# Attention weights turned in four quarters of 32 rows, both pairs at the beginning of each round, with a third place for turned weights

## The reference, cut to what matters

```
s = einsum('bnqkgd,bnskd->bnkgqs', q, kb) * (HEAD_DIM_2 ** -0.5)
s = where(mask, s + bias, NEG_INF_2)
m = maximum(max(s, axis=-1), sink)
p = exp(s - m)
p = p / (sum(p, axis=-1) + exp(sink - m))
o = einsum('bnkgqs,bnskd->bnqkgd', p, vb)
return o * silu(gate)
```

## Time and profile before

| | us |
|---|---|
| median of three runs | 1177.78 |
| lowest and highest | 1177.29, 1177.83 |
| the profiled execution | 1178.13 |
| its span, from the first to the last instruction | 1176.3 |
| TensorE busy | 1164.8 |
| VectorE busy | 676.3 |
| GpSimd busy | 456.2 |
| ScalarE busy | 358.3 |

### The profile page before, as it was taken

How to read it: one execution, slowest core, us unless ns; L and a number is a source line. 1 busy time by engine, 2 the same in 40 slices (tenths; PEclk the granted TensorE clock), 3 DMA queues, 4 the chain that set the end, 5 groups by cost and what they waited for, 6 DMA issues and landing times.

```text
span 1176.3 us, 16568 instructions
## 1 busy us (share of the span) xinstructions
PE 1164.8 (99%) x6255; PEld 950.7 (81%) x6255; DVE 676.3 (57%) x1249; ACT 358.3 (30%) x720; POOL 456.2 (39%) x437
## 2 busy tenths in 40 slices
PE   9999999999999999999999999999999999999997
PEld 6888888888888878887878788888988887777786
DVE  5645557333277403067777874894698335555568
ACT  7312122100011212545674631241111134443322
POOL 3424222233342224354666765304224224454534
PEclk9999999999999999999999999999999999999999
DMA  8321121443212122301114241232111220142113
GB/s 240 116 73 45 36 81 36 129 151 120 95 36 72 64 72 81 100 25 27 46 42 133 64 172 62 84 131 66 50 62 39 65 67 1 37 161 83 37 37 143
DMA packets 75072, 93.53 MB, mean 80 GB/s; under 512 B 13937, under 2 KB 54089, under 8 KB 74482
## 3 DMA queue, kind: packets, MB, share of 16 engines
q1 hardware_dynamic: 67270, 88.73, 22.7%
q10 hardware_dynamic: 7724, 3.74, 1.2%
HBM read 75.11 MB, written 18.92 MB: 80 GB/s over the span
## 4 chain that ended last, share of the span: by engine, by line
PE 96%; DVE 1%; POOL 1%; issue 1%; ACT 0%; DVEq 0%; POOLq 0%; ACTq 0%
PE bank L890 24%; PE bank L892 23%; PE bank L891 23%; PE bank L1183 4%; PE bank L1162 3%; PE wide L1176 2%; PE wide L1352 2%; PE bank L1130 1%; PE bank L1119 1%; PE bank L1326 1%; PE wide L892 1%; PE wide L891 1%; PE wide L890 1%; PE wide L1339 1%; PE bank L1107 1%; PE wide L1326 1%
## 5 line engine op out<-in xcount | busy, mean ns | idle before, releaser
L661 POOL CAST whi<-wraw 128x2048 fp32r<-128x2048 f32 x31 | 58.7, 1894 | 453.5 <-PE bank L892 403.7
L890 PE MATMUL bank<-u_hi,wlo 128*128 128x512 f32 x488 | 190.4, 390 | 0.0
L892 PE MATMUL bank<-u_hi,whi 128*128 128x512 f32 x488 | 189.9, 389 | 0.0
L891 PE MATMUL bank<-u_lo,whi 128*128 128x512 f32 x488 | 189.9, 389 | 0.0
L663 POOL TENSOR_TENSOR wlo<-wraw,whi 128x2048 fp32r<-128x2048 f32 x32 | 153.1, 4785 | 3.0 <-ACT whi L2429 0.5
L890 PE MATMUL bank<-x_hi,wlo 128*128 128x512 f32 x312 | 123.4, 395 | 0.0
L892 PE MATMUL bank<-x_hi,whi 128*128 128x512 f32 x312 | 121.6, 390 | 0.0
L891 PE MATMUL bank<-x_lo,whi 128*128 128x512 f32 x312 | 121.5, 389 | 0.0
L890 PEld LDWEIGHTS bank<-u_hi,wlo 128*128 128x128 f32 x488 | 91.6, 188 | 19.8 <-POOL wlo L663 0.8
L892 PEld LDWEIGHTS bank<-u_hi,whi 128*128 128x128 f32 x488 | 91.6, 188 | 19.1
L891 PEld LDWEIGHTS bank<-u_lo,whi 128*128 128x128 f32 x488 | 91.6, 188 | 18.9
(11 more groups left out here) (375 smaller groups left out, 2450.8 us busy)
## 6 DMA issues: line engine op xcount, KB each, us to landing
wraw<-in_w_in SPq DMA_DIRECT2D x26, 1024.0 KB, 5.4
wraw<-in_w_out SPq DMA_DIRECT2D x12, 1024.0 KB, 5.1
xr<-in_x SPq DMA_DIRECT2D x8, 512.0 KB, 7.2
hst<-in_x SPq DMA_DIRECT2D x4, 1024.0 KB, 5.0
hpool<-hst SPq DMA_DIRECT2D x4, 1024.0 KB, 4.2
smz<-mzs SPq DMA_DIRECT2D x16, 256.0 KB, 2.0
h<-hpool SPq DMA_DIRECT2D x4, 1024.0 KB, 7.6
resid<-h SPq DMA_DIRECT2D x8, 512.0 KB, 2.6
```

The lines of the kernel that those rows point to most:

```text
L661: g_.tensor_copy(whi[w % 2][:, :, :], wraw[:, :, :]).then_inc(s["w_hi"], 1)
L890: pe.matmul(ps, al, bh, start=(k == 0), stop=False)
L891: pe.matmul(ps, ah, bl, start=False, stop=False)
L892: return pe.matmul(ps, ah, bh, start=False, stop=(k == nk - 1))
```

## The change

Four things are edited, all in the attention.

- **Quarters.** `turn_p` makes of each 128 x 128 square four transposes of 32 rows, in four row groups, to the banks 0, 1, 6 and 7. Each of these banks holds both pairs of a round (columns 0 to 255 the even pair, from 256 the odd one). Banks 0 and 1 are now one tensor `both`; ScalarE's copy reads `both`, VectorE's reads `wide1` (banks 6 and 7). A copy still moves 384 (or 256) columns. `weigh` reads the turned weights in four runs of 32 columns (`pT_of`).
- **Both pairs at the beginning of each round**, in all rounds, on TensorE, VectorE and ScalarE. Both copies wait until both pairs are turned (`t_pt`), and the scores of the next even and odd pair wait until ScalarE and VectorE have copied both pairs.
- **A third place** for turned weights: places go by x % 3 (`turned_place`), so a copy waits for the weighing of the pair three before. The new places are `pTd` and `pTe`.
- **Order within a round.** VectorE does both `row_scale` right behind the scores, ahead of `side_out` and `low_y2`. ScalarE does both `weights` ahead of `side_out` and `high_y2`. GpSimd scales both pairs and splits weights behind them.

```diff
-        yp_lo, cc, ym_lo, x2_lo, y2c, _c, pTc = region(
+        yp_lo, cc, ym_lo, x2_lo, y2c, pTe, pTc = region(
...
-        bank = [ctx.enter_context(nc.psum_tensor(f"bank{i}", [P, 512], F32)) for i in range(4)]
+        both = ctx.enter_context(nc.psum_tensor("both", [P, S], F32))
+        bank = [both[:, 0:512], both[:, 512:S]]
+        bank += [ctx.enter_context(nc.psum_tensor(f"bank{i}", [P, 512], F32)) for i in range(2, 4)]
...
+        def turned_place(x):
+
+            if x % 3 == 0:
+                return pT
+            return ((pTb, pTd) if x < 16 else (pTc, pTe))[x % 3 - 1][:, :, HALF:HALF + BAND]
 
         def turned_half(x, half):
 
-            nb = pair(x)[4]
-            both = pT if x % 2 == 0 else (pTb if x < 16 else pTc)[:, :, HALF:HALF + BAND]
-            return both[:, :, 0:nb * P].rearrange("p i (b h c) -> p h i b c", h=2, c=64)[:, half]
-
-        def turned_bank(x, ps):
-
-            nb = pair(x)[4]
-            return ps[:, 0:2 * nb * 64].rearrange("p (i b c) -> p i b c", i=2, c=64)
+            n = 64 * pair(x)[4]
+            return turned_place(x)[:, half, 0:2 * n].rearrange("p (q m) -> p q m", q=2)
+
+        def turned_banks(x, half):
+
+            n = 64 * pair(x)[4]
+            pairs = (both, wide[1])[half][:, :].rearrange("p (q m) -> p q m", q=2)
+            return pairs[:, :, 256 * (x % 2):256 * (x % 2) + n]
+
+        def pT_of(x, i, b):
+
+            n = pair(x)[4]
+            rows = turned_place(x)[:, :, 0:128 * n].rearrange("p h (q m c) -> p h q m c", q=2, c=32)
+            return rows[:, :, :, i * n + b, :]
...
-            for x in range(32):
-                scale_p(x)
-                if x + 2 < 32:
-                    sinks(x + 2)
-                if x < 4:
-                    split_part(W_Q1, x)
-                elif 8 <= x < 16 and x % 2:
-                    split_part(W_O2, (x - 8) // 2)
-                elif x >= 16 and x % 2:
-                    split_part(W_O2 + 1 + (x - 16) // 8, x % 8 // 2)
+            for x0 in range(0, 32, 2):
+                for x in (x0, x0 + 1):
+                    scale_p(x)
+                    if x + 2 < 32:
+                        sinks(x + 2)
+                if x0 < 4:
+                    split_part(W_Q1, x0)
+                    split_part(W_Q1, x0 + 1)
+                elif 8 <= x0 < 16:
+                    split_part(W_O2, (x0 - 8) // 2)
+                elif x0 >= 16:
+                    split_part(W_O2 + 1 + (x0 - 16) // 8, x0 % 8 // 2)
...
-                base = (6, 4)[x % 2] if x < 16 else (0, 6)[x % 2]
-                halves = [take(base + half, ("a_pT", "v_pT")[half], x + 1) for half in range(2)]
+                if x % 2 == 0:
+                    for half in range(2):
+                        for q in range(2):
+                            take(6 * half + q, ("a_pT", "v_pT")[half], x + 2)
                 for i in range(2):
                     pe.wait_ge(s["g_nm"], 2 * x + i + 1)
                     for b in range(nb):
-                        for half in range(2):
-                            rows, c = slice(64 * half, 64 * half + 64), (i * nb + b) * 64
-                            mm = pe.transpose(halves[half][:, c:c + 64],
+                        c = 256 * (x % 2) + 32 * (i * nb + b)
+                        for q in range(4):
+                            rows = slice(32 * q, 32 * q + 32)
+                            mm = pe.transpose(bank[(0, 1, 6, 7)[q]][:, c:c + 32],
                                               sp[rows, x % 2, i, BAND - (nb - b) * P:BAND - (nb - b - 1) * P],
-                                              cst[rows, C_ID + 64 * half:C_ID + 64 * half + 64])
+                                              cst[rows, C_ID + 32 * q:C_ID + 32 * q + 32])
...
                 turn_p(x0)
-                if x0 >= 16:
-                    turn_p(x0 + 1)
+                turn_p(x0 + 1)
                 if x0:
                     weigh(x0 - 2)
                     weigh(x0 - 1)
                 if x0 + 2 < 32:
                     pair_scores(x0 + 2)
                     pair_scores(x0 + 3)
-                if x0 < 16:
-                    turn_p(x0 + 1)
                 if x0 == 16:
                     pe.wait_ge(s["v_y2lo"], 8)
                 for x in (x0, x0 + 1):
...
-                        ve.wait_ge(s["t_pt"], 2 * x - 2)
+                        ve.wait_ge(s["t_pt"], 4 * x - 4)
...
-                ps = filled(ve, "t_pt", 2 * x + 2, "v_pT", x + 1)
-                if x >= 2:
-                    ve.wait_ge(s["t_pv"], x - 1)
-                ve.tensor_copy(turned_half(x, 1), turned_bank(x, ps)).then_inc(s["v_pT"], 1)
+                ve.wait_ge(s["t_pt"], 4 * (x // 2 * 2 + 2))
+                if x >= 3:
+                    ve.wait_ge(s["t_pv"], x - 2)
+                ve.tensor_copy(turned_half(x, 1), turned_banks(x, 1)).then_inc(s["v_pT"], 1)
...
                 if x0 < 32:
                     turned(x0)
-                if 16 <= x0 < 32:
                     turned(x0 + 1)
                 if x0:
                     gate_out(x0 - 2)
...
                 if x0 + 2 < 32:
                     pair_scores(x0 + 2)
                     pair_scores(x0 + 3)
-                if x0 < 16:
-                    turned(x0 + 1)
+                    row_scale(x0 + 2)
+                    row_scale(x0 + 3)
                 if x0 in SIDE_OUT:
                     side_out(SIDE_OUT[x0])
-                if x0 + 2 < 32:
-                    row_scale(x0 + 2)
                 for i in PIECES.get(x0, ()):
                     low_y2(8 + i)
-                if x0 + 2 < 32:
-                    row_scale(x0 + 3)
                 if x0 + 1 in SIDE_OUT:
...
-                ps = filled(ac, "t_pt", 2 * x + 2, "a_pT", x + 1)
-                if x >= 2:
-                    ac.wait_ge(s["t_pv"], x - 1)
-                ac.activation(turned_half(x, 0), turned_bank(x, ps), ACT.Copy).then_inc(s["a_pT"], 1)
+                ac.wait_ge(s["t_pt"], 4 * (x // 2 * 2 + 2))
+                if x >= 3:
+                    ac.wait_ge(s["t_pv"], x - 2)
+                if x == 2:
+                    ac.wait_ge(s["v_y2lo"], 8)
+                ac.activation(turned_half(x, 0), turned_banks(x, 0), ACT.Copy).then_inc(s["a_pT"], 1)
...
-            for x in range(33):
-                if x < 16 or x < 32 and x % 2 == 0:
-                    turned(x)
-                if x >= 16 and x % 2 == 0 and x < 32:
-                    turned(x + 1)
-                for i in PIECES.get(x, ()):
-                    high_y2(8 + i)
-                if x in SIDE_OUT:
-                    side_out(SIDE_OUT[x])
-                if x + 2 < 32:
-                    weights(x + 2)
+            for x0 in range(0, 34, 2):
+                if x0 < 32:
+                    turned(x0)
+                    turned(x0 + 1)
+                if x0 + 2 < 32:
+                    weights(x0 + 2)
+                    weights(x0 + 3)
+                for x in (x0, x0 + 1):
+                    if x in SIDE_OUT:
+                        side_out(SIDE_OUT[x])
+                    for i in PIECES.get(x, ()):
+                        high_y2(8 + i)
```

More of the change, by code:

```diff
@@ L210, in build @@
             [("glu", [P, 2, GPAD], F32), ("_h", [P, 6 * S - 2 * GPAD - 4], F32), ("agb", [P, 2, S], F32)],
-            [("_b", [P, 2 * SL - 2 * S], F32), ("pTb", [P, 2, S], F32)],
+            [("_b", [P, 2 * SL - 4 * S], F32), ("pTd", [P, 2, S], F32), ("pTb", [P, 2, S], F32)],
         )
@@ L1351, in weigh @@
                     for i in range(2):
-                        mm = pe.matmul(ps[64 * i:64 * i + 64, 0:P], vt[:, lo + b, g * HD2:(g + 1) * HD2],
-                                       pT_of(x, i)[:, b * P:(b + 1) * P], start=(b == 0), stop=(b == nb - 1))
+                        mm = pe.matmul(ps[64 * i:64 * i + 64, 0:P].rearrange("p (h q c) -> p h q c", h=2, q=2),
+                                       vt[:, lo + b, g * HD2:(g + 1) * HD2], pT_of(x, i, b),
+                                       start=(b == 0), stop=(b == nb - 1))
                 mm.then_inc(s["t_pv"], 1)
```

8 lines of the change are left out of this document (2 added, 6 removed).

## The result

The changed kernel takes 1183.57 us (median of 4 runs, 1183.42 to 1183.73), against 1177.80 us (4 runs, 1177.29 to 1177.90) before: 5.8 us slower, a ratio of 1.0049, 95% interval [1.0037, 1.0061]. The profiled execution took 1183.42 us with a span of 1181.6, so 5.3 us more than the 1176.3 of the span before.

What follows compares the result with a forecast made beforehand. TensorE, busy 99% of the span, was taken as the bound. Terms 0.7 + 0.75 + 0.1 + 4.4 + 0.5 = +6.4 us on the profiled 1178.13, less 0.35 for the median, gave 1184.2 us; 8-in-10 range 1179.0 to 1190.0.

Steps and rivals of the forecast that it cites:

- Step 1: Transposes in quarters instead of halves: the weight load is the floor, 0.066 us per block, +0.7 us.
- The first rival: Transposes: quarters go four at a time, moving columns the bound, -4.2 in place of +0.7, 1179.3 us; chance 0.13.
- the second: Rival on the transposes: instructions are the bound, +10.9 in place of +0.7, 1194.4 us; chance 0.10.
- Step 2: Both pairs first, shared banks, third place: rounds 4 to 12 0, round 0 +0.75, rounds 2 and 14 +0.1 us.
- S: Start of a round's scores on TensorE, predicted at T + 2.51 us.
- T: Start of a round's transposes on TensorE, from which its other times are counted.
- Step 3: VectorE and ScalarE order: late write-backs stall TensorE's second side group, +4.4 us over six rounds, +0.5 in round 16.
- The third rival: Second side group: bank 3 is not late, +4.4 and +0.5 fall away, 1178.1 us; chance 0.08.

Runs made afterwards that it cites:

- r5: Changed kernel with weight loads of 64 columns instead of 128, the other half of the turned weights left out (timing only): 1178.79 us.
- r3: Changed kernel with squares transposed as two halves of 64 rows instead of four quarters of 32: 1183.99 us.
- r1: Changed kernel with VectorE's side bank write-back put back ahead of the two reciprocals in rounds from 16 on: 1178.10 us.
- r2: Changed kernel with VectorE's old order from round 16 on and ScalarE's write-back ahead of the exponentials in round 16: 1177.52 us.
- r4: Changed kernel without the third place, two places for turned weights as in the kernel before: 1191.99 us.
- r6: Kernel before with only VectorE's write-back moved behind both reciprocals in rounds from 16 on: 1182.84 us.
- r7: Kernel before with the third place for turned weights alone, in pairs from 16 on: 1175.45 us.

## Why the prediction was right, point by point

The forecast was 1184.2 us, and 1183.57 were measured. The waits named in each step show in the rows. Some of the sizes were off, and part of that cancelled by luck.

**Step 1.** The distance of the blocks is 0.062 us (predicted 0.066, the load as the floor), two pairs 0.87 us. r5 shows the load's columns as the cause by halving them, with the number of instructions and the moving columns kept. With that, r3 shows that 64 moving columns in place of 32 add no more than 0.03 us a round. My 4 ns for twice the instructions were not there: +0.7 was 0 or slightly less, since the 12 squares take 0.03 less a round than halves do. The first rival and the second fall with it. For dimensions of 32 or less the Trainium skill (TensorEngine Tiling (Array Packing), section Theoretical Speedup) speaks of up to 4 times. Here nothing of that is reached over two row groups: 12 squares take 0.87 us with four and 0.90 with two. The Trainium skill (TensorEngine Tiling (Array Packing), section Instruction Overhead) gives each matmul some 60 cycles of overhead, which as an estimate from that page would be 0.10 us for the four matmuls of a square. The trace of r5 doesn't agree, with four matmuls and four loads every 0.033 us.

**Step 2.** S came at T + 2.49 (2.51 predicted) and the copies at T + 1.07 and T + 1.85 (1.05 and 1.9). Round 0 costs 0.70 (0.75): TensorE waits for the odd copy with no weighing to cover it.

```profile
989.72 0.45 PE L1336 MATMUL both<-kA,qT 64*64 64x320 f32 x1 [0.93 <-ACT pTb L2544]
```

Rounds 2 and 14 cost 0.08 together (0.1), rounds 4 to 12 gained up to 0.02 each (0).

**Step 3.** The second side group starts at S + 4.93 (5.03 predicted), since TensorE goes on 0.74 after the sum's start and not 0.83. Rounds 20 to 26 are 0.74 to 0.79 longer (0.73), 10.36 to 10.41 us each. The delay against S + 4.10 is 0.83, and there is a term that I didn't have: from the start of the second group to the next transposes it is 2.99 us in the changed kernel (1077.88 to 1080.87) and 2.82 in r1 (1084.97 to 1087.79). TensorE's next matmul comes 0.34 after the first one and not 0.23, and the four behind it 0.23 to 0.24. So a stall of 0.83 cost 0.99, and the two errors, 0.10 too much for the wait and 0.16 left out behind it, nearly cancelled. That is luck.

Round 16 is 0.57 longer (0.5). r2 shows 0.69 for it against r1, since round 16 without the stall is a little shorter than before, 8.81 to 8.89.

Two rounds were wrong. Round 18 is 1.22 longer, for three reasons: the kernel before had no wait inside its scores there (its first side group starts at S + 1.24 and not S + 1.36); the stall costs 0.15 beyond its length; and the changed kernel's sum starts 0.26 after the reciprocal's end, so that TensorE's second group starts at S + 5.28 and not S + 4.93. The profile puts this last wait down to TensorE's group before:

```profile
1066.33 0.17 DVE L2029 RECIPROCAL rcx<-smx 128x2 f32<-128x2 f32 x1 [0.94 <-ACT sp L2535]
1066.76 1.28 DVE L2060 SCALAR_TENSOR_TENSOR res<-res,bank 128x512 f32<-128x512 f32 x2 [0.27 <-PE bank L902]
```

r3 and r5 have this 0.27 in the same place, r4 and r6 don't. It is not what the sum waits for by its semaphores: TensorE had left the group that it reads for the transposes of round 18 at 1059.96, and the residual's tile had landed by DMA at 1055.46. What it is stays open.

Round 28 is only 0.16 longer. I let the row of a full pair stand for pairs 30 and 31, which have 256 keys: their exponentials are shorter, the sum starts at 1118.03 and TensorE waits 0.24:

```profile
1118.77 0.50 PE L900 MATMUL bank<-whi,y2a 128*128 128x512 f32 x1 [0.24 <-DVE res L2060]
```

The six rounds of step 3 come to 4.4 us predicted and 4.4 measured (1.22 for round 18, 3.05 for 20 to 26, 0.16 for 28). That the total fits so well is luck too: 0.5 too little for round 18 and 0.6 too much for round 28.

**The sum.** 0.70 + 0.08 + 4.43 + 0.57, less 0.07 for rounds 4 to 12, is 5.7 in the stretch; 6.4 had been predicted, and what is over is step 1's 0.7. In the span it is 5.3, since the changed kernel came into the attention 0.40 us earlier; that was so at 788 us already, where the two programs are alike. Over the nine kernels this start lies between 987.7 and 988.9 us.

**The third rival** (bank 3 not late) was put at 1178.1 us. r2 is that case made on purpose and took 1177.52. Its size was right within 0.6 us: with bank 3 in time, rounds 18 to 28 are 1.4 us shorter than before (1.2 in the rival's sum). But bank 3 was in time there because both write-backs were put back, and not, as the rival needs, because the exponentials were over sooner: the last reciprocal is at S + 4.10 in r1 as in the changed kernel.

**Two slips in the numbers.** Half way between 0.7 and 10.9 us for the cost of instructions is 5.8, so the upper end of the range should have been 1189.3 and not 1190.0; and the chances of the first and third rival add to 0.21. Neither bears on the outcome.

## What to carry to other kernels

An engine's queue is worth reading for what stands behind a wait. Here a write-back that frees a bank was moved behind a reciprocal that waits for another engine, and a bank wanted every round came 0.8 us late; put it ahead of the wait and it costs nothing. When the waits of two units of work are joined, ask which unit's release now counts: four banks that are free only after both pairs' copies made the odd pair's copy the gate of the scores, and the third place only bought that back. The part of the change that paid, the third place, is worth 2.4 us when it stands alone in the second half.

## What the runs showed of the hardware

- The distance of short transposes follows the columns of their weight load: 0.062 us for a square with 128 columns in the load, whether it goes as four row groups of 32 rows or two of 64, and 0.033 with 64 columns in four row groups. A load lasts 0.13 to 0.14 us by the profile, longer than the distance, so the loads of two squares overlap. The four loads of one square (round 20 of the changed kernel) start within 0.01 us and run beside each other.
- Eight instructions of TensorE (four loads, four matmuls) fit in 0.033 us (r5).
- A stall of TensorE in front of a group of 512-column matmuls costs more than its length. In every round from 16 to 28 in which the second side group waited, in the changed kernel and in r1, r3, r4, r5 and r6, the group took 2.94 to 2.99 us to the next transposes and its second matmul came 0.34 after the first. In every such round without that wait, in r1, r2, r6, r7 and the kernel before, it took 2.81 to 2.82 and 0.23. The extra 0.13 to 0.18 us is the same after 0.1 us of shown idle time as after 1.0, and whether VectorE or ScalarE ended the wait. Why it is so, no run tells.
- The idle time shown is itself less than the delay (0.68 for 0.83): a matmul's row lasts 0.39 us, while the next one starts 0.23 after it, so some 0.16 us of a delay lies under the row before.
- With halves the first distance behind other work is 0.11 us, with quarters 0.08. No run tells why.
